# VectorE's order in a decoder layer's local attention units, and the first chunks of its input projection

## The chip, the cores and the metric

The kernel runs on one core of a Trainium2 chip. The time is device microseconds (us) of one execution. Before the change the median of three runs is 679.45 us (679.43 to 679.52). The engines are TensorE (PE, with its weight loads as PEld), VectorE (DVE), ScalarE (ACT), GpSimd (POOL) and SyncE (SP), which issues most of the DMAs. Each runs its own list of instructions in order, and they meet only at semaphores.

## The reference

One hybrid decoder layer in float32, 512 tokens of width 1024, cut to what matters:

```python
proj = einsum('bsd,dc->bsc', x, w_in)     # q_f k_f v_f | f_logit | q_s k_s v_s | g_f g_s
o_f  = forgetting_attention(q_f, k_f, v_f, cumsum(log_sigmoid(f_logit + b_forget)))   # 8 heads x 64
qs, ks = apply_rope(q_s), apply_rope(k_s)
o_s  = sliding_window_sink_attention(qs, ks, v_s, sinks)   # window 128, 8 q heads, 2 kv heads
#   m = max(max(s), sink); e = exp(s - m); p = e / (sum(e) + exp(sink - m)); out = p @ v
merged = sigmoid(g_f) * (o_f @ w_o_fox) + sigmoid(g_s) * (o_s @ w_o_swa)
h = layer_norm(alpha * x + merged @ w_out)
out = layer_norm(alpha * h + (silu(h @ w_gate) * (h @ w_up)) @ w_down)
```

## The kernel before

Every float32 product is made of three passes of TensorE over operands that are split in two: a rounded high part, and the low part that is left (x minus its rounding). ScalarE rounds the high part (`slab_hi`, line 643), VectorE subtracts for the low part (`slab_lo`, line 982). The passes are high x high, high x low and low x high (`mm3`, lines 1643 to 1645).

The weights come in slabs of 128 x 1024, numbered n. Slabs 0, 1, 4, 5 are the local queries q_s, 2 and 3 hold the local keys and values with the forget logits, 6 to 9 the global queries q_f (`N_QF` = 6), 10 to 13 the global keys k_f (`N_KF` = 10), 14 to 17 the global values (`N_V` = 14), then gates, output projections and the FFN. SyncE loads a slab, ScalarE rounds it, VectorE makes its low part three slabs ahead of its use, and TensorE runs its 24 products over eight chunks of 128 input rows.

The first two slabs start differently. The input x comes in eight chunks of 128 x 512 and the slabs in halves of 128 x 512, interleaved in one DMA queue. `first_slabs` runs chunk by chunk over both slabs, n = 0 and then n = 1, so that each chunk of x serves six products (lines 1832, 1835, 1840). ScalarE rounds each chunk (line 785) and each half (line 779).

Local attention runs in eight units a = 0 to 7, one for each head, and unit a starts at step 6 + a (`unit_step`). In step n each engine goes through a fixed list. Written for one unit, the stages are:

- TensorE: the unit's scores inside slab n (line 1676; from unit 1 on they wait for `exp_done` of the unit before). One step later its transposes (line 1706), which wait for its normalised probabilities. One more step later the product with the values (line 1720), which waits for the low part of the transposed probabilities.
- VectorE, in the order of one step: `maxima(n-6)` on the scores (line 1153, eight instructions), `take(n-1)`, which makes the second part of what slab n-1 left in PSUM (line 1049 for q_f, line 990 for k_f), `sum_o(n-8)`, the low part `ptl` of unit n-7's transposed probabilities (line 990), rotary work in steps 7 and 8 only, `normalise(n-6)` after the exponentials, and the low part of slab n+3 (line 982).
- ScalarE, in the order of one step: `take(n-1)`, the first part of slab n-1 (line 689 for q_f, two instructions; line 696 for k_f, four), `o_low`, the high part `pth` of the transposed probabilities (line 741), `exps(n-6)` (lines 718 and 720; it waits for `max_done`), for every second unit one more copy (line 754), and the rounding of slab n+3 (line 643).

VectorE's `take(n-1)` always waits for ScalarE's `take(n-1)` (`qk_hi`). TensorE's slab n waits for `take(n-2)`, since it writes the PSUM bank that was taken:

```python
elif 8 <= n < N_V:
    pe.wait_ge(qk_taken, n - 7)
```

The order is written by hand: the loops over n in the blocks of the engines are the program. Nothing reorders it.

Of the kernel before, what the change touches and what calls it, by code (L numbers as in the profile page):

```python
# [31 lines left out]
P = 128  # L32
# [12 lines left out]
KC = D // P  # L45
# [4 lines left out]
N_VK = (2, 3)  # L50
N_QF = 6
# [8 lines left out]
VK_W = 2 * KV_W + HEADS  # L60
FIRST = 4

HALF_AFTER = (0, 3)
RAW = 2
SPL = 4
AHEAD = SPL - 1
# [144 lines left out]
def program(nc, xT, x, slabs, vk_slabs, gu, wdn, rope, rope_tok, sel, b_forget, sinks, ln1_g, ln1_b, ln2_g, ln2_b, out):  # L211
    ctx = ExitStack()
    with ctx:
# [5 lines left out]
        def sem(name):  # L219
            return ctx.enter_context(nc.semaphore(name))  # L220
# [95 lines left out]
        x_landed = [sem(f"x_landed{c}") for c in range(KC)]  # L316

        part_landed = [sem(f"part_landed{k}") for k in range(4)]
        part_hi = sem("part_hi")
        part_lo = sem("part_lo")  # L320
        first_landed = {n: sem(f"first_landed{n}") for n in range(2, FIRST)}
# [158 lines left out]
        def _(sp):  # L480
# [8 lines left out]

            for c in range(KC):  # L490
                sp.dma_start(x_raw[:, c, :], xT[c]).then_inc(x_landed[c], 16)
                if c in HALF_AFTER:
                    q = HALF_AFTER.index(c)
                    for n in range(2):
                        sp.dma_start(first_raw[:, n, PART[q]], slabs[n][:, PART[q]])\
                            .then_inc(part_landed[2 * n + q], 16)
# [138 lines left out]
        def _(act):  # L635
# [140 lines left out]
            def part_of_slab_hi(n, q):  # L776

                act.wait_ge(part_landed[2 * n + q], 16)
                act.activation(slot(sh, n)[:, PART[q]], raw_of(n)[:, PART[q]], ACT.Copy)\
                    .then_inc(hi_ready if q else part_hi, 1)  # L780


            for c in range(KC):
                act.wait_ge(x_landed[c], 16)
                act.activation(xh[:, c, :], x_raw[:, c, :], ACT.Copy).then_inc(x_hi, 1)
                if c in HALF_AFTER:
                    for n in range(2):
                        part_of_slab_hi(n, HALF_AFTER.index(c))
            for n in range(2, AHEAD + 1):
                slab_hi(n)  # L790

# [186 lines left out]
        def _(dve):  # L978
# [334 lines left out]
                last.then_inc(hT_ready, 1)  # L1313

            def part_of_slab_lo(n, q):
                dve.wait_ge(hi_ready if q else part_hi, n + 1)
                low(slot(sl, n)[:, PART[q]], raw_of(n)[:, PART[q]], slot(sh, n)[:, PART[q]])\
                    .then_inc(lo_ready if q else part_lo, 1)

            for c in range(KC):  # L1320
                dve.wait_ge(x_hi, c + 1)
                dve.tensor_tensor(xl[:, c, :], x_raw[:, c, :], xh[:, c, :].bitcast(F32), ALU.subtract)\
                    .then_inc(x_lo, 1)
                if c in HALF_AFTER:
                    for n in range(2):
                        part_of_slab_lo(n, HALF_AFTER.index(c))
            for n in range(2, AHEAD + 1):
                slab_lo(n)
            def rope_rest(n):
# [5 lines left out]
                        rope_add(k)  # L1335

            for n in range(1, N_WOUT + KC - WOUT_TAIL + 1):
                for a in units_at(n, 0):
                    maxima(a)
                if n - 1 in N_QS:  # L1340
                    rope_cosine(n - 1, N_QS.index(n - 1))
                if n == N_QS[-2] + 1:
# [3 lines left out]
                if n == N_VK[1] + 1:  # L1346
                    forget_logits()
                    rotate_keys()
                    slab_lo(n - 1 + AHEAD)
                take(n - 1)  # L1350
                for a in units_at(n, 2):
                    sum_o(a)
                if n == N_CUM + 1:
# [16 lines left out]
                    merge(n - 1 - N_WO)  # L1370
                if n - 1 in N_QS[:2]:
                    rope_add(N_QS.index(n - 1))
                if n != N_VK[1]:
                    slab_lo(n + AHEAD)
                if n >= LATE_STEP:
                    late_slab_lo(n - LATE_STEP)
# [263 lines left out]
        def _(pe):  # L1640
# [177 lines left out]


            def first_slabs():  # L1820
                for c in range(KC):
                    for n in range(2):
                        dst = ps[:, proj_bank(n), :]
                        wh, wl = cut(n, c * P, (c + 1) * P)
                        start, stop = c == 0, c == KC - 1
                        if n == 0:
                            pe.wait_ge(x_hi, c + 1)
                        if c == 0:
                            pe.wait_ge(part_hi, n + 1)
                        elif c == KC // 2:  # L1830
                            pe.wait_ge(hi_ready, n + 1)
                        pe.matmul(dst, wh, xh[:, c, :], start=start, stop=False)
                        if n == 0:
                            pe.wait_ge(x_lo, c + 1)
                        pe.matmul(dst, wh, xl[:, c, :], start=False, stop=False)
                        if c == 0:
                            pe.wait_ge(part_lo, n + 1)
                        elif c == KC // 2:
                            pe.wait_ge(lo_ready, n + 1)
                        last = pe.matmul(dst, wl, xh[:, c, :], start=False, stop=stop)  # L1840
                        if stop:
                            last.then_inc(slab_done, 1)

            def rows(n, c, lhs, bank, q, t, start, stop):

# [289 lines left out]
```

## Time and profile before

| | |
|---|---|
| median of 3 runs | 679.45 us (679.43 to 679.52) |
| profiled execution | 679.46 us, of which its span is 677.7 us |
| busy: PE, DVE, ACT, POOL | 665.8, 540.3, 392.2, 50.8 us |
| granted TensorE clock | 0.998 of full speed |
| chain that ended last | PE 89%, DVE 5%, ACT 2%, issue 2%, DMA 1% |

The times in the rows are from the span's start. A row of the timeline gives start, duration, engine, line, operation, output and inputs, how many instructions were merged, and in brackets how long the engine was idle before it and what ended that. A matmul of 512 columns is shown some 0.39 us long, but the next one starts 0.23 us after it, since they overlap; a wait of TensorE is best read from the distance between two starts.

### The profile page before, as it was taken

What the parts mean: (1) busy time and instruction counts of PE and PEld (TensorE: products, weight loads), DVE (VectorE), ACT (ScalarE), POOL (GpSimd) and SP (SyncE); (2) the same over time, 40 slices, a digit from 0 to 9 for tenths busy, and PEclk for the clock granted to TensorE, in tenths of its full rate; (3) what the DMA queues carried; (4) which work ended last, traced back from release to release, by engine and by line L of the source; (5) the groups of instructions that cost most, each with busy time, mean ns of one, the idle gap of its engine ahead of it and who ended that gap; (6) DMA issues with size and microseconds to landing.
All of it is one profiled execution on the core that took longest, in us unless ns stands there. A gap on an engine that the chain in (4) does not pass through costs nothing.

```text
span 677.7 us, 10965 instructions
## 1 busy us (share of the span) xinstructions
PE 665.8 (98%) x4034; PEld 594.8 (88%) x4034; DVE 540.3 (80%) x1021; ACT 392.2 (58%) x728; POOL 50.8 (7%) x74
## 2 busy tenths in 40 slices
PE   8999999999999999999999999999999999999995
PEld 6977888888888888888899999999999998888884
DVE  5579998767876226655989998888998889998888
ACT  5669687467766244524436555554554558767740
POOL 2102111111001011110200000000000000000000
PEclk9999999999999999999999999999999999999999
DMA  8236667876512886886021244334334327987302
GB/s 314 78 116 171 186 176 213 216 183 164 121 63 95 317 205 168 220 270 200 0 79 60 102 150 155 104 128 155 110 122 155 127 92 249 372 258 208 108 31 93
DMA packets 29560, 107.38 MB, mean 158 GB/s; under 512 B 3616, under 2 KB 3744, under 8 KB 26784
## 3 DMA queue, kind: packets, MB, share of 16 engines
q1 hardware_dynamic: 24624, 79.60, 34.1%
q0 software_dynamic: 4896, 27.28, 16.6%
q8 instruction: 21, 0.34, 0.2%
q14 instruction: 19, 0.16, 0.1%
HBM read 104.77 MB, written 25.17 MB: 192 GB/s over the span
## 4 chain that ended last, share of the span: by engine, by line
PE 89%; DVE 5%; ACT 2%; issue 2%; DMA 1%; POOL 0%; DVEq 0%; SPq 0%; ACTq 0%
PE ps L1643 12%; PE ps L1645 12%; PE ps L1644 12%; PE ps L1960 10%; PE ps L1962 10%; PE ps L1961 10%; PE ps L2028 5%; PE ps L2030 5%; PE ps L2029 5%; PE ps L1720 2%; PE ps L1706 2%; ACT rope L659 1%; PE ps L1681 1%; PE ps L1676 1%; DVE sl L982 1%
## 5 line engine op out<-in xcount | busy, mean ns | idle before, releaser
L982 DVE TENSOR_TENSOR sl<-raw,sh 128x1024 fp32r<-128x1024 f32 x46 | 56.3, 1225 | 43.6 <-ACT sh L643 43.5
L1960 PE MATMUL ps<-hTh,sh 128*128 128x256 f32 x320 | 90.6, 283 | 0.0
L1961 PE MATMUL ps<-hTh,sl 128*128 128x256 f32 x320 | 90.6, 283 | 0.0
L1962 PE MATMUL ps<-hTl,sh 128*128 128x256 f32 x320 | 90.6, 283 | 0.0
L1643 PE MATMUL ps<-xh,sh 128*128 128x512 f32 x208 | 83.6, 402 | 1.1 <-DVE q_f L1049 1.1
L1645 PE MATMUL ps<-xl,sh 128*128 128x512 f32 x208 | 81.3, 391 | 0.0
L1644 PE MATMUL ps<-xh,sl 128*128 128x512 f32 x208 | 81.1, 390 | 0.0
L643 ACT ACTIVATE sh<-raw 128x1024 fp32r<-128x1024 f32 x46 | 48.9, 1064 | 35.6 <-PE ps L1645 22.5
L1960 PE MATMUL ps<-vt,sh 128*128 128x256 f32 x240 | 68.1, 284 | 0.2 <-ACT sg L883 0.2
L1962 PE MATMUL ps<-vt,sh 128*128 128x256 f32 x240 | 67.9, 283 | 0.0
L1961 PE MATMUL ps<-vt,sl 128*128 128x256 f32 x240 | 67.9, 283 | 0.0
L1960 PEld LDWEIGHTS ps<-hTh,sh 128*128 128x128 f32 x320 | 61.4, 192 | 0.0
L1961 PEld LDWEIGHTS ps<-hTh,sl 128*128 128x128 f32 x320 | 61.4, 192 | 0.0
L1962 PEld LDWEIGHTS ps<-hTl,sh 128*128 128x128 f32 x320 | 61.4, 192 | 0.0
L990 DVE TENSOR_TENSOR sl<-raw_f_odd,sh 128x1024 fp32r<-128x1024 f32 (+1 forms) x40 | 43.6, 1090 | 12.8 <-ACT sh L873 12.5
L873 ACT ACTIVATE sh<-raw_f_odd 128x1024 fp32r<-128x1024 f32 (+1 forms) x40 | 38.0, 951 | 19.4 <-DVE raw_f_odd L1440 15.9
L873 ACT ACTIVATE sh<-raw_f_even 128x1024 fp32r<-128x1024 f32 (+1 forms) x40 | 37.9, 950 | 17.0 <-DVE raw_f_even L1440 14.0
L1643 PEld LDWEIGHTS ps<-xh,sh 128*128 128x128 f32 x208 | 39.1, 188 | 9.1 <-issue 2.3
L1645 PEld LDWEIGHTS ps<-xl,sh 128*128 128x128 f32 x208 | 39.0, 188 | 8.6
L1960 PEld LDWEIGHTS ps<-vt,sh 128*128 128x128 f32 x240 | 46.1, 192 | 0.4 <-ACT sg L883 0.4
L990 DVE TENSOR_TENSOR sl<-raw_f_even,sh 128x1024 fp32r<-128x1024 f32 (+1 forms) x40 | 43.4, 1087 | 3.7 <-ACT sh L873 3.4
L1962 PEld LDWEIGHTS ps<-vt,sh 128*128 128x128 f32 x240 | 46.1, 192 | 0.0
(255 smaller groups left out, 1747.6 us busy)
## 6 DMA issues: line engine op xcount, KB each, us to landing
raw<-in_slabs SPq DMA_DIRECT2D x46, 512.0 KB, 4.3
raw_f_even<-in_gu SPq DMA_DIRECT2D x10, 1280.0 KB, 5.4
raw_f_odd<-in_gu SPq DMA_DIRECT2D x10, 1280.0 KB, 5.4
item_raw<-tw SPq DMA_DIRECT2D x44, 256.0 KB, 3.1
item_raw<-in_wdn SPq DMA_DIRECT2D x33, 256.0 KB, 5.6
tw<-in_wdn POOLq DMA_DIRECT2D x11, 512.0 KB, 5.6
tw<-tw POOLq DMA_DIRECT2D x22, 256.0 KB, 4.4
x_raw<-in_xT SPq DMA_DIRECT2D x8, 256.0 KB, 5.8
```

The source lines that it names most:

```text
L643: act.activation(slot(sh, n, width_of(n)), raw_of(n), ACT.Copy).then_inc(hi_ready, 1)
L873: act.activation(sh[:, 512 * at_slot:512 * (at_slot + blocks)], raw_f[k % 2][:, first:first + blocks, :].rearrange("p b n -> p (b n)"), AC ...
L982: dve.tensor_tensor(slot(sl, n, w), raw_of(n), slot(sh, n, w).bitcast(F32), ALU.subtract).then_inc(lo_ready, 1)
L990: return dve.tensor_tensor(dst, src, hi.bitcast(F32), ALU.subtract)
L1643: pe.matmul(dst, lh, rh, start=start, stop=False)
L1644: pe.matmul(dst, ll, rh, start=False, stop=False)
L1645: return pe.matmul(dst, lh, rl, start=False, stop=stop)
L1960: pe.matmul(dst, sh[:, w], bh[:, c, :], start=start and c == 0, stop=False, skip_group_check=True)
L1961: pe.matmul(dst, sl[:, w], bh[:, c, :], start=False, stop=False, skip_group_check=True)
L1962: last = pe.matmul(dst, sh[:, w], bl[:, c, :], start=False, stop=c == KC // 2 - 1, skip_group_check=True)
L2028: pe.matmul(dst, lh, rh, start=start, stop=False, skip_group_check=True)
L2029: pe.matmul(dst, ll, rh, start=False, stop=False, skip_group_check=True)
```

## The change

Three parts.

First, in VectorE's list: for steps 7 to 14 `take(n-1)` now stands ahead of the maxima, and the low part of slab 8 moves from the end of step 5 to step 6, behind the maxima of unit 0.

Second, in the first two slabs: the DMA queue carries x chunk 0, slab 0's first half, x chunk 1, slab 1's first half, x chunks 2 and 3, both second halves, and the rest. TensorE runs chunks 0 and 1 of slab 0 ahead of chunks 0 and 1 of slab 1. ScalarE and VectorE follow the order of the queue.

Third: VectorE, not ScalarE, rounds slab 0's first half, with a copy that is its first instruction.

```diff
-HALF_AFTER = (0, 3)
+HALF_BEHIND = {0: ((0, 0),), 1: ((1, 0),), 3: ((0, 1), (1, 1))}
+FIRST_ORDER = ((0, 0), (1, 0), (0, 1), (1, 1)) + tuple((c, n) for c in range(2, 8) for n in range(2))
...
             for c in range(KC):
                 act.wait_ge(x_landed[c], 16)
                 act.activation(xh[:, c, :], x_raw[:, c, :], ACT.Copy).then_inc(x_hi, 1)
-                if c in HALF_AFTER:
-                    for n in range(2):
-                        part_of_slab_hi(n, HALF_AFTER.index(c))
+                for n, q in HALF_BEHIND.get(c, ()):
+                    if (n, q) != (0, 0):
+                        part_of_slab_hi(n, q)
...
+            dve.wait_ge(part_landed[0], 16)
+            dve.tensor_copy(slot(sh, 0)[:, PART[0]], raw_of(0)[:, PART[0]]).then_inc(first_hi, 1)
...
             for n in range(1, N_WOUT + KC - WOUT_TAIL + 1):
+                if N_QF < n <= N_V:
+                    take(n - 1)
                 for a in units_at(n, 0):
                     maxima(a)
+                if n == N_QF:
+                    slab_lo(n - 1 + AHEAD)
...
-                take(n - 1)
+                if not N_QF < n <= N_V:
+                    take(n - 1)
...
-                if n != N_VK[1]:
+                if n not in (N_VK[1], N_QF - 1):
                     slab_lo(n + AHEAD)
...
-                for c in range(KC):
-                    for n in range(2):
+                for c, n in FIRST_ORDER:
```

On VectorE, between the low part of the local keys (`kl_s`) and the probabilities of unit 0, before:

```order
L990 TENSOR_TENSOR kl_s<-ps,kh_s 64x512
L982 TENSOR_TENSOR sl<-raw,sh 128x1024 [waits hi_ready]
L1153 ISA ps,nmax<-ps,masks,sink_neg 128x128 [waits sink_negated,consts_made,scores_done]
...
L999 SCALAR_TENSOR_TENSOR rope_odd<-ps,cs 128x512 [waits rope_done,slab_done]
L1006 TENSOR_TENSOR rope_even<-rope_even,rope_74 128x512 [waits rope_cos,rope_sin]
```

and now:

```order
L991 TENSOR_TENSOR kl_s<-ps,kh_s 64x512
L1154 ISA ps,nmax<-ps,masks,sink_neg 128x128 [waits sink_negated,consts_made,scores_done]
...
L983 TENSOR_TENSOR sl<-raw,sh 128x1024 [waits hi_ready]
L1000 SCALAR_TENSOR_TENSOR rope_odd<-ps,cs 128x512 [waits rope_done,slab_done]
L1007 TENSOR_TENSOR rope_even<-rope_even,rope_74 128x512 [waits rope_cos,rope_sin]
```

The low part of slab 8 (`sl<-raw,sh`) went behind the eight instructions of the maxima.

On VectorE, the start of step 11, the first that takes a slab of global keys (`kl_f`), before:

```order
L982 TENSOR_TENSOR sl<-raw,sh 128x1024 [waits hi_ready]
L1153 ISA ps,nmax<-ps,masks,sink_neg 128x128 [waits exp_done,scores_done]
...
L990 TENSOR_TENSOR kl_f<-ps,kh_f 64x512 [waits qk_hi]
L990 TENSOR_TENSOR kl_f<-ps,kh_f 64x512
L1183 TENSOR_TENSOR o_sum<-ps,o_low 64x512 [waits o_lo,o_low_done]
```

and now:

```order
L983 TENSOR_TENSOR sl<-raw,sh 128x1024 [waits hi_ready]
L991 TENSOR_TENSOR kl_f<-ps,kh_f 64x512 [waits qk_hi]
L991 TENSOR_TENSOR kl_f<-ps,kh_f 64x512
L1154 ISA ps,nmax<-ps,masks,sink_neg 128x128 [waits exp_done,scores_done]
...
L1184 TENSOR_TENSOR o_sum<-ps,o_low 64x512 [waits o_lo,o_low_done]
```

The pair that waits for `qk_hi` stands ahead of the maxima, and the maxima are queued behind its wait. Steps 7 to 10 read the same with `q_f` in place of `kl_f`.

On TensorE, the first nine products, before (`xh`, `xl`: parts of x; `sh`, `sl`: parts of the slab):

```order
L1832 MATMUL ps<-xh,sh 128x512 [waits part_hi,x_hi]
L1835 MATMUL ps<-xl,sh 128x512 [waits x_lo]
L1840 MATMUL ps<-xh,sl 128x512 [waits part_lo]
L1832 MATMUL ps<-xh,sh 128x512 [waits part_hi]
L1835 MATMUL ps<-xl,sh 128x512
L1840 MATMUL ps<-xh,sl 128x512 [waits part_lo]
L1832 MATMUL ps<-xh,sh 128x512 [waits x_hi]
```

and now:

```order
L1846 MATMUL ps<-xh,sh 128x512 [waits first_hi,x_hi]
L1849 MATMUL ps<-xl,sh 128x512 [waits x_lo]
L1854 MATMUL ps<-xh,sl 128x512 [waits part_lo]
L1846 MATMUL ps<-xh,sh 128x512 [waits x_hi]
L1849 MATMUL ps<-xl,sh 128x512 [waits x_lo]
L1854 MATMUL ps<-xh,sl 128x512
L1846 MATMUL ps<-xh,sh 128x512 [waits part_hi]
```

The second group of three now waits for a chunk of x, and the third for slab 1's half.

## Rows read from the trace of the kernel before

**Rows 1.** The page: the span and the busy time of the engines.

```profile
span 677.7 us, 10965 instructions
...
PE 665.8 (98%) x4034; PEld 594.8 (88%) x4034; DVE 540.3 (80%) x1021; ACT 392.2 (58%) x728; POOL 50.8 (7%) x74
```

**Rows 2.** Timeline of PE, steps 6 to 14 (start, duration, what, idle before).

```profile
41.78 0.63 PE L1681 MATMUL ps<-kl_s,q_s 128*128 128x128 f32 x4
...
47.51 0.39 PE L1645 MATMUL ps<-xl,sh 128*128 128x512 f32 x1
48.48 0.33 PE L1676 MATMUL ps<-kh_s,q_s 128*128 128x128 f32 x1 [0.58 <-ACT prob L720]
...
55.68 0.39 PE L1645 MATMUL ps<-xl,sh 128*128 128x512 f32 x1
56.41 0.47 PE L1643 MATMUL ps<-xh,sh 128*128 128x512 f32 x1 [0.35 <-DVE q_f L1049]
...
57.88 0.39 PE L1676 MATMUL ps<-kh_s,q_s 128*128 128x128 f32 x2
...
83.62 0.39 PE L1676 MATMUL ps<-kh_s,q_s 128*128 128x128 f32 x2
...
99.86 0.39 PE L1676 MATMUL ps<-kh_s,q_s 128*128 128x128 f32 x2
...
106.62 0.28 PE L1720 MATMUL ps<-pth,v_s 128*128 128x256 f32 x1
```

**Rows 3.** Timeline of DVE, steps 6 to 13: maxima, q_f, ptl.

```profile
44.63 0.36 DVE L1153 CUSTOM_DVE_ANT_0 ps<-ps,masks,sink_neg 128x128 f32<-128x128 f32 x1
...
53.22 0.35 DVE L1153 CUSTOM_DVE_ANT_0 ps<-ps,masks,sink_neg 128x128 f32<-128x128 f32 x1
...
54.87 1.39 DVE L1049 SCALAR_TENSOR_TENSOR q_f<-ps,q_f 64x512 fp32r<-64x512 f32 x2
...
62.03 0.35 DVE L1153 CUSTOM_DVE_ANT_0 ps<-ps,masks,sink_neg 128x128 f32<-128x128 f32 x1
...
70.84 0.35 DVE L1153 CUSTOM_DVE_ANT_0 ps<-ps,masks,sink_neg 128x128 f32<-128x128 f32 x1
...
78.84 0.35 DVE L1153 CUSTOM_DVE_ANT_0 ps<-ps,masks,sink_neg 128x128 f32<-128x128 f32 x1
...
101.47 0.35 DVE L1153 CUSTOM_DVE_ANT_0 ps<-ps,masks,sink_neg 128x128 f32<-128x128 f32 x1
...
105.09 1.15 DVE L990 TENSOR_TENSOR ptl<-ps,pth 128x512 fp32r<-128x512 f32 x2
```

**Rows 4.** Timeline of ACT: q_f of step 7; exponentials and what follows them, step 11.

```profile
53.12 1.20 ACT L689 ACTIVATE q_f<-ps 64x512 fp32r<-64x512 f32 x2
...
88.71 0.30 ACT L718 ACTIVATE esink<-nmax,sink_sb 128x4 f32<-128x4 f32 x1
...
90.50 0.23 ACT L720 ACTIVATION_READ_ACCUMULATOR prob<-ps,nmax 128x1 f32 x1
90.59 0.66 ACT L754 ACTIVATE o_s<-o_sum 128x512 fp32r<-128x512 f32 x1
91.11 1.09 ACT L643 ACTIVATE sh<-raw 128x1024 fp32r<-128x1024 f32 x1
92.06 2.41 ACT L696 ACTIVATE kh_f<-ps 64x512 fp32r<-64x512 f32 x4
```

**Rows 5.** Timeline of the start, all engines.

```profile
6.57 0.63 ACT L779 ACTIVATE sh<-first_raw 128x512 fp32r<-128x512 f32 x1 [1.81 <-DMA first_raw<-in_slabs]
...
7.25 0.50 PE L1832 MATMUL ps<-xh,sh 128*128 128x512 f32 x1 [1.05 <-ACT sh L779]
7.34 1.96 ACT L785 ACTIVATE xh<-x_raw 128x512 fp32r<-128x512 f32 x3
...
10.02 0.39 PE L1832 MATMUL ps<-xh,sh 128*128 128x512 f32 x1
```

**Rows 6.** Stretches of the start: busy time, granted clock, DMA share, GB/s.

```profile
5.00:10.00 5.00, 3.91 (x12) 2.26 (x13) 3.16 (x6) 3.16 (x6) 0.00 (x0) 1.00 0.99 341
```

More of the change, by code:

```diff
@@ L318, in program @@
         part_landed = [sem(f"part_landed{k}") for k in range(4)]
+        first_hi = sem("first_hi")
         part_hi = sem("part_hi")
@@ L491, in _ @@
                 sp.dma_start(x_raw[:, c, :], xT[c]).then_inc(x_landed[c], 16)
-                if c in HALF_AFTER:
-                    q = HALF_AFTER.index(c)
-                    for n in range(2):
-                        sp.dma_start(first_raw[:, n, PART[q]], slabs[n][:, PART[q]])\
-                            .then_inc(part_landed[2 * n + q], 16)
+                for n, q in HALF_BEHIND.get(c, ()):
+                    sp.dma_start(first_raw[:, n, PART[q]], slabs[n][:, PART[q]]).then_inc(part_landed[2 * n + q], 16)
             sp.dma_start(cs[:, :, :], rope).then_inc(cs_landed, 16)
@@ L785, in _ @@
                 act.activation(xh[:, c, :], x_raw[:, c, :], ACT.Copy).then_inc(x_hi, 1)
-                if c in HALF_AFTER:
-                    for n in range(2):
-                        part_of_slab_hi(n, HALF_AFTER.index(c))
+                for n, q in HALF_BEHIND.get(c, ()):
+                    if (n, q) != (0, 0):
+                        part_of_slab_hi(n, q)
             for n in range(2, AHEAD + 1):
@@ L1315, in part_of_slab_lo @@
             def part_of_slab_lo(n, q):
-                dve.wait_ge(hi_ready if q else part_hi, n + 1)
+                if q:
+                    dve.wait_ge(hi_ready, n + 1)
+                elif n:
+                    dve.wait_ge(part_hi, 1)
+                else:
+                    dve.wait_ge(first_hi, 1)
                 low(slot(sl, n)[:, PART[q]], raw_of(n)[:, PART[q]], slot(sh, n)[:, PART[q]])\
                     .then_inc(lo_ready if q else part_lo, 1)
+            dve.wait_ge(part_landed[0], 16)
+            dve.tensor_copy(slot(sh, 0)[:, PART[0]], raw_of(0)[:, PART[0]]).then_inc(first_hi, 1)
             for c in range(KC):
@@ L1323, in _ @@
                     .then_inc(x_lo, 1)
-                if c in HALF_AFTER:
-                    for n in range(2):
-                        part_of_slab_lo(n, HALF_AFTER.index(c))
+                for n, q in HALF_BEHIND.get(c, ()):
+                    part_of_slab_lo(n, q)
             for n in range(2, AHEAD + 1):
@@ L1820, in first_slabs @@
             def first_slabs():
-                for c in range(KC):
[L1822 to L1842, printed above, removed]
+                for c, n in FIRST_ORDER:
+                    dst = ps[:, proj_bank(n), :]
+                    wh, wl = cut(n, c * P, (c + 1) * P)
+                    start, stop = c == 0, c == KC - 1
+                    if n == 0:
+                        pe.wait_ge(x_hi, c + 1)
+                    if c == 0:
+                        pe.wait_ge(part_hi if n else first_hi, 1)
+                    elif c == KC // 2:
+                        pe.wait_ge(hi_ready, n + 1)
+                    pe.matmul(dst, wh, xh[:, c, :], start=start, stop=False)
+                    if n == 0:
+                        pe.wait_ge(x_lo, c + 1)
+                    pe.matmul(dst, wh, xl[:, c, :], start=False, stop=False)
+                    if c == 0:
+                        pe.wait_ge(part_lo, n + 1)
+                    elif c == KC // 2:
+                        pe.wait_ge(lo_ready, n + 1)
+                    last = pe.matmul(dst, wl, xh[:, c, :], start=False, stop=stop)
+                    if stop:
+                        last.then_inc(slab_done, 1)
             def rows(n, c, lhs, bank, q, t, start, stop):
```

## The prediction

> **What bounds the kernel now.** I read the page first: TensorE is busy for 665.8 of 677.7 us [rows 1]. A microsecond is won only where TensorE waits, and one is lost wherever a new wait is put ahead of it. So I looked for TensorE's waits by the distance between two starts of its matmuls, 0.23 us where nothing is late. Up to step 14 there are two places. At the start it gets its second slab half only at 7.25 us [rows 5]. In the local units it waits four times. At 48.48 the scores of unit 1 come 0.97 us after the matmul before them: 0.74 us lost, and ScalarE's exponentials of unit 0 released them. At 56.41 slab 8 comes 0.73 us after slab 7's last matmul: 0.50 us lost, to VectorE's q_f [rows 2]. Slabs 9 and 10 wait in the same way, three such waits in all, some 1.6 us together.
>
> Then I read VectorE's and ScalarE's timelines over these steps, to see whether VectorE has room. It has none: the maxima of units 1, 2, 3 and 4 begin at 53.22, 62.03, 70.84 and 78.84 [rows 3], and VectorE is idle nowhere between. The steps last 8.81, 8.81 and 8.00 us, and that is VectorE's own work. TensorE's period with nothing late is 8.12 us: the scores of units 5 and 7, two steps apart, begin at 83.62 and 99.86 [rows 2]. The third view is the order on the two engines: who stands behind whom. From it come two chains into TensorE. One is take(n-2) to slab n, the chain that is late now. The other is maxima(a), exponentials(a), scores(a+1). The change shortens the first by putting the pair ahead of the maxima, and lengthens the second by the same 1.42 us.
>
> **Part 1a, slab 8's low part behind the maxima of unit 0.** Unit 0's scores end at 41.78 + 0.63 = 42.41 [rows 2], but its maxima start at 44.63 [rows 3], behind the low part of slab 8, which first waits for ScalarE. Now they start at 42.45: 2.18 us earlier. The exponentials follow by as much, so their end, which released 48.48, comes at about 46.25. TensorE is ready for the scores at 47.51 + 0.23 = 47.74. The wait of 0.74 us goes. The low part of slab 8 is then made by 45.3; slab 8 starts after 54. ScalarE's queue behind the exponentials (rotary copies, slab 9, two more copies, q_f of slab 6) moves up by 2.18 too.
>
> **Part 1b, steps 7 to 10.** ScalarE's q_f of slab 6 ended at 53.12 + 1.20 = 54.32 [rows 4]; now 52.14. VectorE's pair follows at 52.17 and takes 1.42 (1.39 in [rows 3], plus the handover). So slab 8 waits no more. But the maxima of unit 1 begin at 53.59, later than their 53.22 of before though everything in front of them is 2 us early. Maxima last 1.65 us (53.22 to 54.87 [rows 3]), the exponentials 2.02 (88.71 to 90.50 + 0.23 [rows 4]): they end at 57.3, and the scores of unit 2 start there. TensorE would be ready at 57.88 - 0.74 - 0.50 = 56.64. So it has a new wait of 0.7 us and is 0.6 us ahead of before, not 1.24.
>
> From here VectorE sets the pace with its own work, which the change does not make less: maxima of unit 2 at 53.59 + 8.81 = 62.40, of unit 3 at 71.21. In step 9 one thing is new. From maxima to the end of `ptl` there are now 3.36 us (101.47 to 105.09 + 1.15 [rows 3] is 4.77, less 1.41 for the pair that no longer stands between), but maxima, exponentials and semaphores take 3.7: VectorE waits 0.35 us for the exponentials. Maxima of unit 4: 71.21 + 8.00 + 0.35 = 79.56, exponentials at 81.2, done at 83.25, scores of unit 5 at 83.3 against 83.62 [rows 2]. TensorE is 0.3 us ahead. At 78.84 against 79.56 the lead on VectorE is already gone.
>
> **Part 1c, steps 11 to 13, where the sum turns.** ScalarE's first part of a slab of global keys is four copies, 2.41 us [rows 4]. Before, the maxima did not wait for it. Now all of this stands in one line: exponentials(a) 1.88 until ScalarE is free (88.71 to 90.59), for every second unit 0.52 (90.59 to 91.11), slab rounding 0.95 (91.11 to 92.06), keys 2.41, VectorE's pair 1.41, maxima 1.65, two handovers 0.1: 8.4 us, or 8.9 in step 11 to 12, where that extra copy stands [rows 4]. TensorE's period is 8.12. Exponentials of unit 5 at 81.2 + 8.4 = 89.6, of unit 6 at 98.5, done at 100.5: the scores of unit 7 at 100.6 against 99.86 [rows 2], 0.7 us behind. Maxima of unit 7 then at 98.5 + 1.88 + 0.95 + 2.41 + 1.41 + 0.06 = 105.2, and `ptl` of unit 6, behind them, ends at 108.6. The product with the values of unit 6, before at 106.62 [rows 2], waits for it: 108.6, 2.0 us behind. Behind step 13 no maxima stand until step 19, slab 14 needs only the exponentials of unit 7 (done at 109.0, before TensorE is there at 109.5), and TensorE has nowhere to catch up. Part 1 costs 2.0 us.
>
> **Part 2, the first slabs.** The third transfer lands at 6.55 and the fourth at 7.3 at the latest (ScalarE starts on it at 7.34 [rows 5]); now the third is x chunk 1 and the fourth slab 1's half. ScalarE rounds chunk 1 at 6.57 to 7.20, TensorE starts at 7.25 as before. Its second product needs VectorE's low part of the chunk: 7.25 + 0.70, so 8.0. The third has all it needs at 8.3; slab 1's chunk 0 follows at 8.55 (rounded by 7.95) and its third product is free at 9.0. The twelfth product ends the block, and chunk 2 begins at about 9.95 against 10.02 [rows 5]. I take a gain of 0.1 us. Bounds: 0.2 if each wait costs TensorE nothing, and a loss of 0.3 if the landings move by as much, since nothing in the trace shows chunk 1 third in the queue. Behind it TensorE has all chunks in time, so this counts in full.
>
> **Part 3, the copy on VectorE.** It adds one 128 x 512 instruction before VectorE's first low part. The nearest rows are 0.63 us for ScalarE's rounding of the same size [rows 5] and 1.39 for a pair on VectorE, 0.70 each [rows 3]. Below nothing it cannot be. At 0.70 the first product starts at about 4.9, the third at 6.3, and TensorE still waits for the third landing until 7.25. Cost 0, and at most 0.1 if a semaphore is late. What hides it is the landing at 6.55.
>
> **Sum.** -0.1 + 2.0 = 1.9 us. Profiled execution 679.46, which is also the median's 679.45: 681.4 us, slower.
>
> **The rivals.**
> 1. *All four waits go and none comes* (faster). It holds if VectorE's exponentials chain has slack that I do not see, for example if the maxima run sooner because ScalarE's q_f and keys are done well before. For it: before, ScalarE is idle for stretches in these steps, and the wait that the rows name is VectorE's q_f. Against it: VectorE has no idle time between 53.22 and 78.84. 679.46 - 0.74 - 1.6 - 0.1 = 677.0 us. It decides if the exponentials of unit 1 end before 56.6.
> 2. *Only the query steps are as I say, the keys cost nothing.* If the line of 8.4 to 8.9 us is below TensorE's period, for example because ScalarE gets slab rounding done during VectorE's wait, TensorE keeps its 0.3 to 0.6: 679.46 - 0.4 - 0.1 = 679.0 us.
> 3. *The waits themselves cost more.* Each engine that now waits starts its next instruction late; the pair that released 56.41 ended at 54.87 + 1.39 = 56.26, so 0.15 us passed before TensorE moved [rows 2, 3]. Two or three new waits per step, seven steps, 0.05 to 0.1 each beyond my handovers: 1 to 1.5 more, 682.9 us.
> 4. *TensorE's clock.* New waits of up to 1.5 us might let the clock fall from 2.4 to 1.2 GHz. Against it: from 5 to 10 us TensorE was busy for only 3.91 of 5.00 us and the granted clock was 1.00 [rows 6], which is the upper level. Every 24 products at the lower level would cost 5.5 us more (24 x 0.23), so over 685 us. I give it 1 in 100. The Trainium skill warns of this in "TensorE: Matmul & The Clock Gate", section "HAM oscillation — how this bites in real kernels": a kernel whose matmuls wait between bursts falls back to the low clock again and again. By that rule the change would be worse than I say; the trace so far speaks against it, as the row shows.
>
> **How the numbers follow.** My forecast, 680.8 to 682.2, has 0.50; rival 3, up to 683.4, 0.13; in between the forecast and rival 2, 679.4 to 680.8, 0.10; rival 2, 678.1 to 679.4, 0.12; rival 1, below 678.1, 0.14; the clock 0.01. A measurement of this kernel tells 0.2% from no change, which is 1.36 us. Slower than 680.81: 0.50 + 0.13 + 0.01 + a little of the middle, 0.66. Faster than 678.09: 0.15. The same: 0.19. The range takes in rival 2 and rival 3: 678.3 to 683.3.
>
> **What would show it.** In the profile after, TensorE's wait at slabs 8 to 10 for q_f and at the scores of unit 1 should be gone, and line 1676's successor should wait for ScalarE's exponentials in units 2 to 7, longest in 2 and 7, and the product with unit 6's values for `ptl`, by over 1 us. ScalarE should be idle before its exponentials in every step, and VectorE before `kl_f` in steps 11 to 13. The scores of unit 2 should come near 57.3, of unit 5 near 83.3, of unit 7 near 100.6, and chunk 2 near 9.95. I am wrong if scores of units 2 to 5 start without a wait (rival 1), or if the distance of the exponentials in steps 11 to 13 is 8.1 (rival 2). The start is wrong if TensorE reaches chunk 2 after 10.1.

## The result, and the profile after

The changed kernel is slower, as forecast.

| | before | after |
|---|---|---|
| median of 6 runs each | 679.44 us (678.89 to 680.29) | 682.60 us (681.87 to 683.49) |
| ratio | 1 | 1.0048, 95% interval 1.0035 to 1.006 |
| profiled execution | 679.46 | 682.08, of which the span is 680.4 |
| mean granted TensorE clock of it | 0.998 | 0.996 |
| last matmul starts at | 669.52 | 672.20 |

The forecast was 681.4. The profiled execution moved by 2.62 us and lies 0.7 above it; the medians moved by 3.2, and the median of 682.60 lies 0.4 above the band that the prediction calls its forecast, 680.8 to 682.2, in the one that it gave to rival 3. The page after, span and busy time, answers to [rows 1]: TensorE is busy 0.8 us more in a span 2.7 us longer, so most of the loss is waiting.

```profile
span 680.4 us, 10965 instructions
...
PE 666.6 (98%) x4034; PEld 595.0 (87%) x4034; DVE 541.6 (80%) x1022; ACT 391.5 (58%) x727; POOL 50.7 (7%) x74
```

The waits of TensorE after (engine, tile and line that waits, who ended it: us in total, times, longest):

```profile
PE ps L1691 <- ACT prob L720: 2.3, 4, 1.0
PE ps L1735 <- DVE ptl L991: 1.3, 1, 1.3
...
PE ps L1846 <- ACT xh L786: 0.8, 1, 0.8
PE ps L1849 <- DVE xl L1331: 0.2, 1, 0.2
```

No wait for q_f is left. The scores (line 1691, was 1676) now wait for the exponentials four times (units 2, 3, 4 and 7; by the distance of the starts units 5 and 6 are held too, by 0.16 and 0.24 us), and the product with the values of unit 6 (line 1735, was 1720) once, for 1.3 us. The timeline of TensorE after, which answers to [rows 2]:

```profile
47.67 0.63 PE L1691 MATMUL ps<-kh_s,q_s 128*128 128x128 f32 x4
57.38 0.73 PE L1691 MATMUL ps<-kh_s,q_s 128*128 128x128 f32 x4 [0.98 <-ACT prob L720]
...
83.29 0.73 PE L1691 MATMUL ps<-kh_s,q_s 128*128 128x128 f32 x4
...
100.75 0.73 PE L1691 MATMUL ps<-kh_s,q_s 128*128 128x128 f32 x4 [0.61 <-ACT prob L720]
...
109.09 0.39 PE L1735 MATMUL ps<-pth,v_s 128*128 128x256 f32 x1 [1.31 <-DVE ptl L991]
```

These are scores of units 1, 2, 5, 7 and the values of unit 6. Against before they come 0.81, 0.50 and 0.33 us early, then 0.89 and 2.47 us late. Nearly all of the loss is made between 83 and 109 us; the last matmul is 2.68 late. The timeline of ScalarE after, from step 11 (answers to [rows 4]):

```profile
89.69 0.30 ACT L718 ACTIVATE esink<-nmax,sink_sb 128x4 f32<-128x4 f32 x1 [1.10 <-DVE nmax L1154]
...
91.59 0.63 ACT L754 ACTIVATE o_s<-o_sum 128x512 fp32r<-128x512 f32 x1
92.11 1.06 ACT L643 ACTIVATE sh<-raw 128x1024 fp32r<-128x1024 f32 x1
93.06 2.40 ACT L696 ACTIVATE kh_f<-ps 64x512 fp32r<-64x512 f32 x4
...
98.69 0.30 ACT L718 ACTIVATE esink<-nmax,sink_sb 128x4 f32<-128x4 f32 x1 [1.61 <-DVE nmax L1154]
...
107.17 0.30 ACT L718 ACTIVATE esink<-nmax,sink_sb 128x4 f32<-128x4 f32 x1 [1.10 <-DVE nmax L1154]
```

Exponentials start 9.00 and 8.48 us apart (before 8.12), and each set waits for the maxima. ScalarE is busy 58% of the span and still helps to pace the kernel here, because it and VectorE wait for each other. The timeline of VectorE after, one query step and one step of the keys (answers to [rows 3]):

```profile
52.23 1.39 DVE L1050 SCALAR_TENSOR_TENSOR q_f<-ps,q_f 64x512 fp32r<-64x512 f32 x2 [1.04 <-ACT q_f L689]
53.65 0.36 DVE L1154 CUSTOM_DVE_ANT_0 ps<-ps,masks,sink_neg 128x128 f32<-128x128 f32 x1
53.93 0.14 DVE L1154 DVE_READ_ACCUMULATOR2_ANT nmax<- 128x1 f32 x1
...
86.50 1.39 DVE L991 TENSOR_TENSOR kl_f<-ps,kh_f 64x512 fp32r<-64x512 f32 x2 [0.61 <-ACT kh_f L696]
87.92 0.36 DVE L1154 CUSTOM_DVE_ANT_0 ps<-ps,masks,sink_neg 128x128 f32<-128x128 f32 x1
88.31 0.08 DVE L1154 DVE_READ_ACCUMULATOR2_ANT nmax<- 128x1 f32 x1
```

Look at the first read of the accumulator. Behind q_f it starts 0.28 us after the first maximum, behind kl_f 0.39. I had not foreseen that; it is taken up below. And the start after, all engines (answers to [rows 5]):

```profile
4.25 0.43 DVE L1328 CAST sh<-first_raw 128x512 fp32r<-128x512 f32 x1 [4.25 <-DMA first_raw<-in_slabs]
...
7.32 0.50 PE L1846 MATMUL ps<-xh,sh 128*128 128x512 f32 x1 [0.79 <-ACT xh L786]
...
8.04 0.50 PE L1849 MATMUL ps<-xl,sh 128*128 128x512 f32 x1 [0.23 <-DVE xl L1331]
...
9.99 0.39 PE L1846 MATMUL ps<-xh,sh 128*128 128x512 f32 x1
```

### The profile page after: what moved, and what is told of

It reads as the page before. It is cut to its first block, busy times and chain, and to the rows that moved or that the text cites. A ratio compares the mean times of both kernels' runs of the same rounds, so it can differ in the third digit from the quotient of the medians.

```text
span 680.4 us, 10965 instructions
## 1 busy us (share of the span) xinstructions
PE 666.6 (98%) x4034; PEld 595.0 (87%) x4034; DVE 541.6 (80%) x1022; ACT 391.5 (58%) x727; POOL 50.7 (7%) x74
## 4 chain that ended last, share of the span: by engine, by line
PE 87%; DVE 6%; ACT 4%; issue 2%; DMA 1%; DVEq 0%; SPq 0%; ACTq 0%
PE ps L1658 12%; PE ps L1660 12%; PE ps L1659 12%; PE ps L1974 10%; PE ps L1976 10%; PE ps L1975 10%; PE ps L2042 5%; PE ps L2044 5%; PE ps L2043 5%; PE ps L1735 2%; PE ps L1721 1%; DVE ps L1154 1%; ACT prob L720 1%; PE ps L1691 1%; PE ps L1696 1%
## 5 line engine op out<-in xcount | busy, mean ns | idle before, releaser
L1975 PEld LDWEIGHTS ps<-vt,sl 128*128 128x128 f32 x240 | 46.1, 192 | 0.0
```

Source lines behind the costliest of these rows:

```text
L1975: pe.matmul(dst, sl[:, w], bh[:, c, :], start=False, stop=False, skip_group_check=True)
```

## The experiments

Eleven experiments ran, two of them repeats of a kernel, in three groups that each share runs of the kernel before (medians 679.93, 679.53 and 679.48 us). The medians are blurred by something at the start: in a part of the executions the twelve first products take about 1.3 us longer. Six of the thirteen traces show it; of the kernel before no trace does, but the recorded clock of some of its executions points to it. "The clock at the start", below, is about it. So I read the unit steps with a yardstick that leaves the start out: the distance from the first scores of unit 0 to the product with the values of unit 6, in the profiled execution. Where a kernel has two traces, the two agree within 0.01 us. From kernel to kernel it is less exact: "start only" has the unit steps of before and reads 0.13 us more.

| kernel | chunk 2 starts | scores of unit 0 | values of unit 6 | yardstick |
|---|---|---|---|---|
| before | 10.02 | 41.24 | 106.62 | 65.38 |
| after | 9.99 | 41.19 | 109.09 | 67.90 |
| after, second execution | 11.44 | 42.63 | 110.53 | 67.90 |
| maxima first | 11.17 | 42.36 | 105.70 | 63.34 |
| queries only | 11.39 | 42.59 | 107.79 | 65.20 |
| keys only | 11.01 | 42.23 | 107.63 | 65.40 |
| start only | 9.60 | 40.82 | 106.33 | 65.51 |
| after, longer keys | 9.51 | 40.72 | 110.49 | 69.77 |
| maxima first, longer keys | 9.62 | 41.00 | 104.32 | 63.32 |
| best | 9.58 | 41.50 | 104.14 | 62.64 |
| best, second execution | 9.73 | 40.92 | 103.57 | 62.65 |
| best, filled | 11.20 | 42.42 | 105.05 | 62.63 |
| after, halves swapped | 11.46 | 42.73 | 109.89 | 67.16 |

**Maxima first.** The changed kernel with `take` behind the maxima again in every step. Slab 8's low part stays where the change put it, and so does the start.

```diff
-                if N_QF < n <= N_V:
-                    take(n - 1)
...
-                if not N_QF < n <= N_V:
-                    take(n - 1)
+                take(n - 1)
```

> The changed kernel with the take of every step put back behind the maxima; slab 8's low part stays behind unit 0's maxima, and the new start stays. Theory A (the pair ahead of the maxima lengthens the line maxima, exponentials, next scores): the wait of 0.74 us at 48.48 is gone, no scores wait for exponentials, unit 1's maxima begin near 51.0, one wait of some 0.6 us for q_f is left at slab 10, unit 7's scores begin near 97.7: 2.1 us below before, 677.3 us. Theory B (the loss comes from the start or from something later than step 14): the time stays near the changed kernel's, 681.5 to 682.5 us. Theory C (the early low part of slab 8 is what costs): slower than the changed kernel or the same.

Measured: median 678.50 us (677.06 to 678.83, 9 runs), ratio 0.9967 (0.9954 to 0.998). The four at a mean clock of 0.997 or more took 677.06 to 677.38, the five at 0.995 took 678.50 to 678.83. Of TensorE's waits in the unit steps one is left:

```profile
PE ps L1655 <- DVE q_f L1050: 0.4, 1, 0.4
```

So the one-line move of slab 8's low part is the good part of the change. It takes 2.04 us out of the yardstick (65.38 to 63.34): the wait at the scores of unit 1 and two of the three for q_f, since VectorE's queue, being 2 us early, reaches q_f in time. The takes in front cost 4.56 us (63.34 to 67.90).

**Queries only** and **keys only.** The whole change, but with `take` in front of the maxima only in the steps of the query slabs, or only in those of the key slabs.

```diff
-                if N_QF < n <= N_V:
+                if N_QF < n <= N_KF:
...
-                if not N_QF < n <= N_V:
+                if not N_QF < n <= N_KF:
```

```diff
-                if N_QF < n <= N_V:
+                if N_KF < n <= N_V:
...
-                if not N_QF < n <= N_V:
+                if not N_KF < n <= N_V:
```

> The changed kernel with the take ahead of the maxima in steps 7 to 10 only. Theory A: scores of units 2 to 5 as in the changed kernel (57.4, 66.1, 74.9, 83.3), then no further loss: unit 7's scores near 99.4, the product with unit 6's values near 106.2, 0.4 us below before: 679.0 us. If the query steps carried the loss (theory D): 681.5 us or more.

> The changed kernel with the take ahead of the maxima in steps 11 to 14 only. Theory A: units 1 to 4 as with the maxima first (unit 4's scores near 73.1), but exponentials 8.5 to 9.0 us apart in steps 11 to 13; the lead of 2.1 us is used up at the product with unit 6's values, which waits 1.3 us or more for ptl: 0.0 to 0.3 us above before, 679.5 to 679.8 us. Theory D (the query steps carry the loss): 677.3 us.

Measured: 679.66 us (678.60 to 680.92, 12 runs), ratio 0.9995 (0.9985 to 1.0005), and 679.44 us (678.90 to 681.02, 12 runs), ratio 0.9994 (0.9984 to 1.0004). Both are no different from before by the times. The waits of the first in the unit steps, and then two of the three of the second (it has one more of 0.4 us for q_f at slab 10, as "maxima first" has):

```profile
PE ps L1691 <- ACT prob L720: 1.7, 3, 1.0
```

```profile
PE ps L1735 <- DVE ptl L991: 1.3, 1, 1.3
...
PE ps L1691 <- ACT prob L720: 0.3, 1, 0.3
```

By the yardstick, against "maxima first", the query steps alone cost 1.86 us (65.20), the key steps alone 2.06 (65.40), both together 4.56. The line in the key steps has the same length alone (exponentials at 88.24, 97.23 and 105.70, 8.99 and 8.47 apart), but there it starts from a lead: its first exponentials wait 0.48 us for the maxima, in the kernel after 1.10. I take it that this is why the two parts add up to less than the whole (3.92 against 4.56); no run tests it.

**Start only.** The kernel before with the new start (part 2 and 3 of the change), and nothing moved in the unit steps.

```diff
-                if N_QF < n <= N_V:
-                    take(n - 1)
...
-                if n == N_QF:
-                    slab_lo(n - 1 + AHEAD)
...
-                if not N_QF < n <= N_V:
-                    take(n - 1)
+                take(n - 1)
...
-                if n not in (N_VK[1], N_QF - 1):
+                if n != N_VK[1]:
```

> The kernel before with only the new start (order of the transfers, order of the first products, the copy on VectorE); VectorE's order of before in all steps. Theory A: chunk 2 begins at 9.99 against 10.02, everything behind it as before: 0.0 to 0.1 us below before, 679.4 us. Theory B (the start costs): 1 us or more above before.

Measured: 680.32 us (678.61 to 681.06, 12 runs), ratio 1.0005 (0.9994 to 1.0015). The profiled one took 679.20, with chunk 2 at 9.60. Chunk 2 is 0.42 us earlier than before here and 0.03 in the profile after. The median shows nothing of it: the interval holds no change. The six traces of the new start without the long beginning have chunk 2 anywhere from 9.51 to 9.99, and before has one trace, 10.02. So the new start seems to gain 0.0 to 0.5 us, and a single execution can't size it.

**After, longer keys**, and **maxima first, longer keys.** One more copy of ScalarE, 128 x 512, behind the four of each of slabs 10 to 12. It writes to a spare tile that nothing reads.

```diff
+                    if n < N_V - 1:
+                        last = act.activation(spare[n - N_KF][:, :], ps[:, b, :], ACT.Copy)
```

> The changed kernel with one more ScalarE copy of 0.6 us (128x512 into a spare tile) behind each of the first three key slabs' copies, ahead of the signal that VectorE's pair waits for (steps 11 to 13). Theory A: in this order ScalarE's keys stand in the line to the next exponentials, so each of the three copies is paid in full: exponentials 9.1 to 9.6 us apart, and 1.8 us more than the changed kernel, 683.9 us where the changed kernel has 682.1. Rival (ScalarE has room in these steps, 58% busy, and the line is set by VectorE alone): no more than 0.3 us above the changed kernel.

> The same three extra copies of 0.6 us, but with the maxima first (the order of the first experiment). Theory A: ScalarE's keys do not stand ahead of the maxima here, so the copies fall into ScalarE's waits: 0 to 0.4 us above the first experiment, 677.3 to 677.7 us. Rival: ScalarE's work counts in either order, 1.8 us above the first experiment, 679.1 us.

Measured: 684.98 us (683.23 to 687.03, 6 runs), ratio 1.0077 (1.0058 to 1.0096), against 677.47 us (677.04 to 677.79, 7 runs), ratio 0.9968 (0.9957 to 0.9979). ScalarE in the first, timeline of the key steps:

```profile
80.78 0.30 ACT L721 ACTIVATE esink<-nmax,sink_sb 128x4 f32<-128x4 f32 x1 [1.01 <-DVE nmax L1157]
...
89.87 0.30 ACT L721 ACTIVATE esink<-nmax,sink_sb 128x4 f32<-128x4 f32 x1 [1.60 <-DVE nmax L1157]
...
99.48 0.30 ACT L721 ACTIVATE esink<-nmax,sink_sb 128x4 f32<-128x4 f32 x1 [1.60 <-DVE nmax L1157]
...
108.57 0.30 ACT L721 ACTIVATE esink<-nmax,sink_sb 128x4 f32<-128x4 f32 x1 [1.60 <-DVE nmax L1157]
```

The same of the second:

```profile
86.41 0.30 ACT L721 ACTIVATE esink<-nmax,sink_sb 128x4 f32<-128x4 f32 x1
...
94.53 0.30 ACT L721 ACTIVATE esink<-nmax,sink_sb 128x4 f32<-128x4 f32 x1
...
102.65 0.30 ACT L721 ACTIVATE esink<-nmax,sink_sb 128x4 f32<-128x4 f32 x1
```

This is the clearest test of the line. The same 0.6 us of work lengthens the distance of the exponentials from 9.00 and 8.48 to 9.61 and 9.09 where the keys stand in front of the maxima, and leaves it at 8.12 where they stand behind. The yardstick grows by 1.87 us (67.90 to 69.77), three times 0.62, in the first, and not at all in the second (63.34, 63.32). The sum in the first is larger than I expected, and the reason is rival 4, a fall of the clock. Its TensorE waits 1.92 us for `ptl` at 110.49, and the stretches behind that wait (busy time, granted clock, DMA share, GB/s) read:

```profile
108.00:110.00 2.00, 0.56 (x3) 0.14 (x1) 1.94 (x7) 1.43 (x7) 0.00 (x0) 1.00 0.90 143
110.00:112.00 2.00, 1.51 (x10) 1.42 (x11) 1.75 (x7) 2.00 (x7) 0.00 (x0) 0.88 0.70 131
112.00:114.00 2.00, 2.00 (x6) 1.47 (x5) 1.83 (x3) 1.97 (x5) 0.80 (x1) 0.50 0.04 8
114.00:116.00 2.00, 2.00 (x12) 1.80 (x11) 1.59 (x3) 1.46 (x4) 0.00 (x0) 0.76 1.03 131
```

The clock is at its lower level, 1.2 GHz, from 112 to 114 and in a part of the stretches on both sides, and that adds 1.5 us between unit 6's values and the end (last matmul 564.58 us behind them; in the two executions of after 563.11 and 562.96). In the kernel after the wait in the same place is 1.31 us, and the granted clock of the stretches from 106 to 114 is 1.00. That the wait caused the fall is my reading of one trace: three of the six executions have a mean clock of 0.994 or less, the others 0.996 to 0.998.

**After, halves swapped.** VectorE's second part of q_f and k_f starts with partitions 64 to 127 and ends with 0 to 63.

```diff
-                    for g in range(2):
+                    for g in (1, 0):
```

> The changed kernel with the two instructions of VectorE's pair (line 1050 for q_f, 991 for k_f) in the other order, so that the pair for q_f ends with a write to partitions 64 to 127 and the pair for k_f with one to partitions 0 to 63. In the changed kernel the second of the maxima starts 0.39 us after the first behind kl_f and 0.28 behind q_f. Theory H (the accumulator read behind the first maxima is held when the write before it began in another quadrant of partitions): the two change places, 0.28 behind kl_f and 0.39 behind q_f. Rival: the distance hangs on the tile (kl_f, q_f) or on the wait in front of it, and stays 0.39 behind kl_f. The span moves by less than 0.5 us either way.

Measured in one execution: 682.81 us, with the long start (chunk 2 at 11.46). VectorE's timeline behind q_f and behind kl_f:

```profile
53.78 1.39 DVE L1050 SCALAR_TENSOR_TENSOR q_f<-ps,q_f 64x512 fp32r<-64x512 f32 x2 [1.04 <-ACT q_f L689]
55.10 0.34 DVE L1154 CUSTOM_DVE_ANT_0 ps<-ps,masks,sink_neg 128x128 f32<-128x128 f32 x1
55.46 0.08 DVE L1154 DVE_READ_ACCUMULATOR2_ANT nmax<- 128x1 f32 x1
...
87.99 1.39 DVE L991 TENSOR_TENSOR kl_f<-ps,kh_f 64x512 fp32r<-64x512 f32 x2 [0.60 <-ACT kh_f L696]
89.30 0.34 DVE L1154 CUSTOM_DVE_ANT_0 ps<-ps,masks,sink_neg 128x128 f32<-128x128 f32 x1
89.57 0.13 DVE L1154 DVE_READ_ACCUMULATOR2_ANT nmax<- 128x1 f32 x1
```

The long read has changed sides: 0.36 us behind q_f and 0.27 behind kl_f. So it hangs on which half the pair in front ends with. A second effect was not in my expectation: the first maximum starts 1.32 and 1.31 us after its pair, where it was 1.42 in both. In the key steps both gains add up: exponentials 8.25, 8.77 and 8.24 apart against 8.46, 9.00 and 8.48, and most of the 0.74 us that come off the yardstick (67.90 to 67.16). In the query steps they nearly cancel: the second maximum starts 1.68 us after the pair, where it was 1.70.

**Best**, and the same kernel again. "Maxima first", and two moves more: the rotary low part of slab 5 from step 8 to step 10, so that VectorE reaches q_f of slab 8 in time, and in step 13 the take behind `ptl`. The edit against "maxima first":

```diff
-                    if n == m + 2 + (k >= 2):
+                    if n == (10 if k == 3 else m + 2 + (k >= 2)):
...
-                take(n - 1)
+                if n != N_V - 1:
+                    take(n - 1)
...
+                if n == N_V - 1:
+                    take(n - 1)
```

> The first experiment, with two more moves on VectorE: the low part of the rotated slab 5 (a pair, 1.42 us) goes from step 8 to step 10, since unit 6's scores in step 12 are the first that read it, and in step 13 the take of slab 12 goes behind ptl of unit 6. Theory A: VectorE's own work in step 8 falls from 8.81 to 7.4 us, below TensorE's 8.12, so the wait of 0.6 us at slab 10 is gone, and nothing of it comes back at the product with unit 6's values: 0.5 us below the first experiment, 676.8 us. Rival (that wait is not VectorE's load): the same as the first experiment, 677.3 us.

> The seventh experiment's kernel again, as the partner of the ninth on the same chip: 676.0 to 676.9 us where the clock holds; by theory F some executions 1.2 to 1.5 us above these at a granted clock of 0.995 or lower.

Measured: 676.44 us (676.01 to 676.92, 5 runs), ratio 0.995 (0.9934 to 0.9965); again: 676.53 us (675.92 to 679.70, 12 runs), ratio 0.9966 (0.9953 to 0.9979). TensorE waits nowhere in the unit steps now. It beats both kernels: 3.1 and 2.95 us under before in the two groups, and 6.3 under after in the second. By the yardstick it is 0.70 us better than "maxima first", in both executions, and 2.74 better than before: that is all that the waits in these steps were worth. The 0.70 is the wait at slab 10; the move in step 13 gave nothing, for from unit 7's scores to unit 6's values there are 6.76 us with it and without it. The 2.74 is more than the 0.74 and 1.6 us that the prediction read. The other 0.4 us fits the four waits too: behind each, TensorE's next matmuls take 0.1 us more. From the first scores of unit 1 (line 1676) to the next four (line 1681) there are 0.57 us behind the wait at 48.48, and 0.46 in "best", where no wait stands ahead. Three of the twelve took 678.92 to 679.70 at clocks of 0.996 to 0.998, and I have no trace of such a one: unexplained.

**Best, filled.** Three products of ones, 128 x 128, behind the first three products of the kernel; their result is overwritten unread. They were to keep TensorE busy where the clock at the start might fall.

```diff
+                    if (c, n) == (0, 0):
+                        for _ in range(3):
+                            pe.matmul(ps[:, VK_BANKS.start, 0:P], ones[:, :], ones[:, :], start=True, stop=True)
```

> The seventh experiment's kernel with three small 128x128 matmuls (of ones, results not used) on TensorE between its third and fourth product, where it otherwise waits for x chunk 1 until about 7.2 us. Theory F (the granted clock drops from 1.00 to 0.50 near 8 us in some executions because TensorE waits at the start, and costs 1.2 to 1.5 us then): no execution is of the long kind, granted clock over the span at least 0.996 in each, the median 676.1 to 676.5 us, and no lower than the seventh's undisturbed executions. Rival G (the drop comes from elsewhere and is a coin at launch): the share of executions at 0.995 or lower is the same as in the other kernels of this call. If the fillers themselves delay chunk 1's products: 0.2 to 0.4 us more in every execution.

Measured: 676.44 us (676.39 to 677.75, 5 runs), ratio 0.9957 (0.9944 to 0.997). Inconclusive: the kernel without the filling showed no long start by its clock either, in 17 executions, so there was nothing to prevent. The one profiled here, the 677.75, has chunk 2 at 11.20, but the filling itself took part in that:

```profile
6.98 1.48 PE L1859 MATMUL ps<-ones 128*128 128x128 f32 x6
8.12 0.77 PE L1846 MATMUL ps<-xh,sh 128*128 128x512 f32 x1
```

ScalarE had rounded chunk 1 by 6.76, and TensorE came to it only at 8.12, behind the filling; in "best" it began at 6.50 and 7.05. So about 1.1 us of the lateness is the filling in this execution. The other four took 676.39 to 676.58, so it does not always cost that.

**After again.** The changed kernel unaltered, to see its spread beside "best".

> The changed kernel again, on the chip of the ninth and tenth: by theory A 681.9 to 682.1 us where the clock holds and 683.1 to 683.5 where it drops; 5.5 to 6 us above the tenth experiment at the same clock.

Measured: 682.81 us (681.86 to 685.30, 6 runs), ratio 1.0054 (1.0037 to 1.007). Its yardstick is 67.90 both times, so the loss in the unit steps repeats within 0.01 us, while chunk 2 lies at 11.44 instead of 9.99.

**The clock at the start.** "Maxima first", the stretches from 4 to 12 us (its execution took 678.50):

```profile
4.00:6.00 2.00, 1.55 (x6) 0.80 (x5) 1.54 (x3) 0.02 (x1) 0.00 (x0) 1.00 0.82 238
6.00:8.00 2.00, 1.40 (x4) 0.72 (x4) 0.78 (x2) 1.26 (x2) 0.00 (x0) 0.91 1.01 330
8.00:10.00 2.00, 2.00 (x6) 1.52 (x6) 1.93 (x3) 1.89 (x3) 0.00 (x0) 0.50 1.03 391
10.00:12.00 2.00, 2.00 (x8) 1.65 (x7) 2.00 (x4) 1.88 (x4) 0.00 (x0) 0.73 1.06 413
```

In the kernel after the same stretches had 1.00 throughout, with TensorE busy 1.03 of 2.00 us from 6 to 8. Here it is 0.50 from 8 to 10, and products start 0.43 us apart instead of 0.23. Of the first six runs of after, three had a mean clock of 0.994 (683.10 to 683.49) and three 0.996 (681.87 to 682.09). Of 32 of before in the first group ten were at 0.994 or under. So I take it for a mixture of two kinds of executions, apart by some 1.3 us. The clock does not sort them cleanly: five more of the 32 took over 680 us at 0.996 to 0.998. "Keys only" has the long start too, with a recorded clock of 0.998, so the distance of the products is the safer sign, and only a trace has it. What decides the kind isn't settled: "best" shows it least by the clock, but before's share also went from 10 of 32 in the first group to one of 17 in the third.

## Why the prediction was right, step by step

**Part 1a** held: scores of unit 1 start at 47.67; the prediction had TensorE ready for them at 47.74. "Maxima first" shows that the same early start also frees two of the q_f waits by itself, which I had given to the takes alone. That was the better change hidden in this one.

**Part 1b** held within 0.1 us: scores of unit 2 at 57.38 (57.3), maxima of unit 4 at 79.56 (79.56), scores of unit 5 at 83.29 (83.3).

**Part 1c** had the right mechanism and the right place. The line was to be 8.9 and 8.4 us and is 9.00 and 8.48. The extra is the long accumulator read behind kl_f, 0.11 us in each of three steps. The "longer keys" pair shows the line to be real: 0.6 us in it costs 0.6, outside it nothing.

**The last term was too small.** I put the values of unit 6 at 108.6, 2.0 us behind; they came at 109.09. Of the 0.49 us, 0.33 is the three reads. Most of the rest is in one place. I had worked out maxima to `ptl` by subtracting 1.41 for the pair that no longer stands between [rows 3]. But kl_f had started together with the last read of the accumulator, at 102.96, and what stands there now does not. VectorE's timeline, before and then after:

```profile
102.96 0.14 DVE L1153 DVE_READ_ACCUMULATOR2_ANT nmax<- 128x1 f32 x1
102.96 1.39 DVE L990 TENSOR_TENSOR kl_f<-ps,kh_f 64x512 fp32r<-64x512 f32 x2
104.37 0.68 DVE L1183 TENSOR_TENSOR o_sum<-ps,o_low 64x512 f32<-64x512 f32 x1
```

```profile
106.99 0.14 DVE L1154 DVE_READ_ACCUMULATOR2_ANT nmax<- 128x1 f32 x1
107.16 0.68 DVE L1184 TENSOR_TENSOR o_sum<-ps,o_low 64x512 f32<-64x512 f32 x1
```

That is 0.17 us; why the one starts with the read and the other behind it, no run here tests. What is left of the profile's 2.68 against my 1.9: 0.07 at the start (a gain of 0.03, not 0.1), 0.10 at the first two value products, which stand 0.22 us apart after the wait instead of 0.12, and 0.11 farther behind. 1.9 + 0.33 + 0.17 + 0.07 + 0.10 + 0.11 = 2.68. The last 0.11 differs between executions: the second one of after does not have it, its last matmul stands 562.96 us behind unit 6's values, against 563.11 in the first and 562.90 before.

**Part 2** was right in order, and its times fit the profiled execution: first product of chunk 1 at 7.32 (7.25), second at 8.04 (8.0), chunk 2 at 9.99 (9.95). That they fit so closely is luck: in the other traces of the same start without the long beginning chunk 1 began between 6.50 and 7.05 and chunk 2 between 9.51 and 9.73. **Part 3**, the copy, cost nothing in the profiled execution, where TensorE still waits 0.79 us for chunk 1 after it; it took 0.43 us, not the 0.70 I took from a subtraction. The Trainium skill says in "VectorE: DVE Perf Modes", section "Mode 2×_2P — use both read ports for one tensor", that an instruction with one input in SBUF can read it through two ports at two results a cycle, and one with two inputs can't; 0.43 against 0.69 for the subtraction of the same size (at 4.59 us) agrees in direction.

**The medians** moved by 0.5 us more than the profile, because three of six executions of after had the long start, by their clock of 0.994; none of the three was traced. I had not reckoned with that. The range holds the median only because it took in rival 3, and not through my own sum.

**The rivals.** Rival 1 fell: VectorE's chain had no slack. But its 677.0 is what "maxima first" and "best" reach by other ways. Rival 2 fell with the distance of 9.00 and 8.48 us. Rival 3 said nearly the right size, 682.9 against the median's 682.60, mostly for a wrong reason: of its 1 to 1.5 us, 0.5 is the held reads (0.11 us at three instructions) and the 0.17 at a fourth, and 0.5 of the median is the long start. The price at each wait exists, 0.1 us as seen under "best", but after the change it counts only at the last wait, since at the others VectorE's and ScalarE's line decides when TensorE goes on. Rival 4 got too small a chance. One stretch at 1.00 in one execution [rows 6] was no evidence about other executions. The second trace of the changed kernel has the fall at the start, and the clocks of before say that before has it too; but in "longer keys", whose wait is 0.6 us longer than this kernel's, it fell in the unit steps and cost 1.5 us. The kernel after stands that near to it. And I had used the section of the Trainium skill too broadly: in "TensorE: Matmul & The Clock Gate", section "HAM oscillation — how this bites in real kernels", the waits of its example are longer than any wait in these traces, so by it the change was not at risk. The fall in "longer keys", behind 1.92 us, came all the same; there the measurement decides.

**Open** are what selects the long start, whether the wait caused the fall in "longer keys", the three slow executions of "best", and one of 685.30 us of the kernel after at a clock of 0.997, where a fall as in "longer keys" would fit the size but no trace shows it.

## What to carry to other kernels

Before you move an instruction ahead of a chain, write down the line that goes round the engines, from one instance of the chain to the next, and compare its length with the bottleneck's period: 8.5 to 9.0 us against 8.12 turned a lead of 0.3 us into a delay of 2.5 in three steps, though each engine had idle time. If an engine is late for its work, look first for what stands in front of the whole queue and could go later (one low part moved won 2 us); shuffling within the full steps took it from one chain and gave it to another. And where differences are under 0.5%, compare distances inside the traces as well as medians.

## What the runs showed of the hardware

**A held accumulator read.** Behind the kl_f pair the first read starts 0.39 us after its maximum, behind the q_f pair 0.28 (87.92 to 88.31, 53.65 to 53.93). With the halves swapped it is 0.27 and 0.36, and the maximum itself starts 0.10 us earlier in both. The code has the difference: both pairs read PSUM in partitions 0 to 63 and then 64 to 127, kl_f is written to the same half, q_f to the other (`half(1 - g)`), and the read writes from partition 0 on. So the maximum is late where the last instruction read the upper half, and the read is late where it wrote the upper half, by about 0.1 us each. The Trainium skill has this rule in "VectorE: DVE Perf Modes", section "Two Vector instructions with no wait between them": an instruction is held until the ones in front have finished if it reads or writes a memory from another quadrant of partitions on than the last one did, and an accumulator's read counts as an instruction of its own. All four cases here agree with it. The distances are the same in every step: 0.27 to 0.28 behind q_f and 0.38 to 0.39 behind kl_f in five traces with the halves in their order, 0.36 to 0.37 and 0.26 to 0.27 in the one with the halves swapped. The three reads of after cost 0.33 us; the rule would have named them, had I applied it to the new neighbours, though not their price.

**The clock can fall behind short waits.** Behind a wait of 1.92 us ("after, longer keys", 108 to 116 us) it went from 1.00 to 0.50 for over 2 us; behind waits of 1.31 and 1.30 us in the same place it stayed at 1.00 in both executions of after. At the start the same kernel's executions differ: in the first trace of after TensorE was busy 1.03 of 2.00 us from 6 to 8 and the clock stayed at 1.00; in the second it was busy 0.79, and the clock went to 0.92 and then 0.50 from 8 to 10.

**A start behind a wait is slow.** The first two value products of unit 6 stand 0.22 us apart behind the wait in after and 0.12 without one in before.
